# A two-block model kernel: the sum of the down products moved from a VectorE addition to an accumulating transfer

## The chip, the cores and the metric

The kernel runs on one core of a Trainium2 chip, in one launch. The metric is the device time of that core in microseconds, from runs of the whole program.

## What is computed

Two transformer blocks of width 2048 over 256 positions, in float32. The change touches the two feed-forward parts only:

```
# first block (w_up 2048 x 8192, w_down 8192 x 2048)
m = rms_norm(h, mlp_pre_gain[l])
z = jnp.square(jax.nn.relu(jnp.einsum("bsd,df->bsf", m, w_up[l])))
z = jnp.einsum("bsf,fd->bsd", z, w_down[l])
h = h + rms_norm(z, mlp_post_gain[l])
...
# second block (w_gu 2048 x 11264, w_down 5632 x 2048)
h2 = rmsnorm(x, g_ffn)
gu = h2 @ w_gu
x = x + (jax.nn.silu(gu[..., :D_FF_2]) * gu[..., D_FF_2:]) @ w_down
```

## The kernel before

Every large product is cut in units of 512 output columns (W) for all 256 positions, held as two tiles of 128 (TT). A unit sums over 2048 inner rows in eight slots (SPU) of two 128-row pieces each. A slot is one 512 KB piece of weights. It goes through a ring of four (RING): SyncE loads it into `raw`, ScalarE rounds it into `w_hi` (L676), VectorE takes the residue `w_lo` (L976), and TensorE does twelve matmuls of 512 columns with it (L399 to L401: w_lo with x_hi, w_hi with x_hi, w_hi with x_lo) into one of two accumulators `acc`. A ring place is free for ScalarE when TensorE has used it (`slot_used`), and free for SyncE when VectorE has made the residue (`lo_ready`). Each engine's program is written out by hand in one order, and semaphores alone order the engines against each other. The names are the buffers': `ev` (two halves of 512 KB) takes the evacuated accumulator, `wide` (2 MB) is the wide accumulator in SBUF, `zz` holds an activated unit, `b_hi` and `b_lo` its transposed and split form, `h` the residual stream, `ssq` the sums of squares that a norm needs.

The MLP (`mlp_block`) runs four blocks over the inner width. Each has four up units and then four down units (NCH is 4). A down unit j adds its part to `wide[:, :, j]`. In the orders of the engines the boundary of a down unit looks like this. ScalarE has rounded the slots up to four ahead (`ticks`), evacuates `acc` into `ev[:, j % 2]` (`evacuate`, L683), waits for `ev_read`, squares `wide[:, :, j]` for the norm that follows the MLP (`squares`, L709; the squares of the first three blocks are overwritten by those of the fourth), and goes on to the next unit's slots:

```
evacuate(j % 2, g + (NCH + j + 1) * SPU, ev[:, j % 2])
act.wait_ge(ev_read, b * NCH + (4 + j + 1))
squares(3, j, wide[:, :, j], b * (2 * NCH) + (24 + 2 * j))
```

VectorE adds `ev` to `wide` (L1187) when the evacuation is counted in `evacuated` and the squares of the block before are done (`squared`), and counts `ev_read`. After the fourth block come the mean square on VectorE (L1004, L1006), the root on GpSimd (`root`, L1391), the residual (L1147) and the transposes of `h` (L416), on which TensorE's next unit depends.

The second feed-forward (`ff_block`) has two blocks of eight up and four down units, which add into `wide` likewise (L1365), and a third of six up and four down units, in which VectorE adds `wide` to `h` (L1345) and then each down unit to `h` directly (L1362). There ScalarE takes no squares; it waits for `ev_read` only where a half of `ev` is to be written again.

GpSimd clears `wide` before each of the two uses (L1451, L1477), loads gains, tables and attention biases by its own DMA queue, and takes the roots.

Of the kernel before, what the change touches and what calls it, by code (L numbers as in the profile page):

```python
# [21 lines left out]
ALU = mybir.AluOpType  # L22
# [3 lines left out]
D = 2048  # L26
# [3 lines left out]
NCH = D // W  # L30
# [45 lines left out]
def build_program(nc, t):  # L76
    ctx = ExitStack()
    with ctx:
# [9 lines left out]
        def sem(name):  # L88
            return ctx.enter_context(nc.semaphore(name))
# [79 lines left out]
        ev_read = sem("ev_read")  # L169
        x_in = [sem(f"x_in{c}") for c in range(NCH)]  # L170
# [493 lines left out]
        def _(act):  # L664
# [142 lines left out]
            def mlp_block(b, last=False):  # L807
                g = G_MLP + b * (2 * NCH * SPU)
                for j in range(NCH):
                    first = isinstance(b, int) and b + j == 0  # L810
                    ticks(g, RING + j * SPU + (RING if first else 0), RING + (j + 1) * SPU)
                    act.wait_ge(rs_ok, 3)
                    act.wait_ge(z_ready, b * NCH + (4 + j))
                    act.wait_ge(ev_read, b * NCH + 4)
                    evacuate(j % 2, g + (j + 1) * SPU, ev[:, j % 2], 2)
                    split(T_MLP + b * (2 * NCH) + 2 * j, b_hi, 4 * j)
                for j in range(NCH):
                    ticks(g, RING + (NCH + j) * SPU,
                          RING + (NCH + j + 1) * SPU - (last and j == NCH - 1))
                    act.wait_ge(z_ready, b * NCH + 8)  # L820
                    act.wait_ge(ev_read, b * NCH + (4 + j))
                    evacuate(j % 2, g + (NCH + j + 1) * SPU, ev[:, j % 2])
                    act.wait_ge(ev_read, b * NCH + (4 + j + 1))
                    squares(3, j, wide[:, :, j], b * (2 * NCH) + (24 + 2 * j))
# [113 lines left out]
            def ff_block(g, b, pairs, down_slots, last):  # L938
                z, r, tr = 32 + b * NCH, 4 + 16 + b * NCH, T_FF + b * (2 * NCH)
                for j in range(2 * pairs):  # L940
                    ticks(g, RING + j * SPU, RING + (j + 1) * SPU)
                    act.wait_ge(rs_ok, 6)
                    if j % 2 == 0:
                        act.wait_ge(z_ready, z + j // 2)
                        act.wait_ge(ev_read, r)
# [5 lines left out]
                for j in range(NCH):  # L951
# [5 lines left out]
                    if j > 1:  # L957
                        if last:
                            act.wait_ge(h_ready, 3 * NCH + j - 1)
                        else:  # L960
                            act.wait_ge(ev_read, r + (j - 1))
# [9 lines left out]
        def _(dve):  # L971
# [194 lines left out]
            def mlp_block(b, last=False):  # L1166
# [10 lines left out]
                if isinstance(b, int) and b == 0:  # L1177
                    dve.wait_ge(wide_zero, 1)
                for j in range(NCH):
                    ticks(g, RING + (NCH + j) * SPU,  # L1180
                          RING + (NCH + j + 1) * SPU - (last and j == NCH - 1))
                    if last and j:
                        dve.wait_ge(squared, b * (2 * NCH) + (24 + 2 * j))
                        gained(j - 1)
                    dve.wait_ge(evacuated, u + (NCH + j + 1))
                    dve.wait_ge(squared, b * (2 * NCH) + (18 + 2 * j))
                    nc.vector.tensor_tensor(wide[:, :, j], wide[:, :, j], ev[:, j % 2], ALU.add  # L1187
                                            ).then_inc(ev_read, 1)
# [152 lines left out]
            def ff_block(g, u, b, pairs, down_slots, last):  # L1341
                for j in range(2 * pairs):
                    ticks(g, RING + j * SPU, RING + (j + 1) * SPU)
                    if last and 1 <= j <= NCH:
                        nc.vector.tensor_tensor(h[:, :, j - 1], h[:, :, j - 1], wide[:, :, j - 1],  # L1345
                                                ALU.add).then_inc(folded, 1)
# [8 lines left out]
                for j in range(NCH):  # L1355
# [3 lines left out]
                    dve.wait_ge(evacuated, u + (2 * pairs + j + 1))  # L1359
                    if last:  # L1360
                        dve.wait_ge(folded, j + 1)
                        nc.vector.tensor_tensor(h[:, :, j], h[:, :, j], ev[:, j % 2], ALU.add  # L1362
                                                ).then_inc(h_ready, 1)
                    else:
                        nc.vector.tensor_tensor(wide[:, :, j], wide[:, :, j], ev[:, j % 2], ALU.add  # L1365
                                                ).then_inc(ev_read, 1)

            dve.wait_ge(wide_zero, 2)
# [8 lines left out]
        def _(pool):  # L1377
# [76 lines left out]
            root(2)  # L1454
            root(3)
# [22 lines left out]
            root(5)  # L1478

# [45 lines left out]
```

## Time and profile before

| | us |
|---|---|
| median of 2 runs | 2595.22 |
| lowest and highest | 2594.0, 2596.45 |
| span of the profiled execution, first to last instruction | 2592.5 |
| TensorE busy in it | 2533.8 |
| VectorE, ScalarE, GpSimd busy | 1472.3, 1235.2, 245.4 |

The profile is of one execution. Its span leaves out what lies before the first and after the last instruction, so it stands a little under the runs' times. Matmuls are pipelined, so the durations of single ones overlap (0.39 us each at a spacing of 0.23). In the rows PE is TensorE, PEld its weight loads, DVE is VectorE, ACT ScalarE, POOL GpSimd and SP SyncE; "idle before" is how long the engine had nothing to do, and the arrow names what ended that. L and a number is a line of the kernel.

### The profile page before, as it was taken

To read this page: it belongs to the slowest core of one execution; us is meant where nothing else is said; L and a number is where in the kernel's file an instruction comes from. 1 tells how busy PE (TensorE), PEld (TensorE's weight loads), DVE (VectorE), ACT (ScalarE), POOL (GpSimd) and SP (SyncE) were. 2 spreads that over 40 slices of the span, in tenths; PEclk is the share of its full clock that TensorE was granted. 3 is DMA by queue.
4 is the path that set the end of the run, shared out by engine and by line. 5 is a ranking of instruction groups with operands and counts; after the bars stand their busy time and mean duration, and the time that the engine had idled before them with its cause. 6 is when DMAs were issued, how large, how long until landed. Compare 5 with 4: busy or idle time off the path is not lost.

```text
span 2592.5 us, 31914 instructions
## 1 busy us (share of the span) xinstructions
PE 2533.8 (98%) x11389; PEld 2096.6 (81%) x11389; DVE 1472.3 (57%) x1548; ACT 1235.2 (48%) x1509; POOL 245.4 (9%) x199
## 2 busy tenths in 40 slices
PE   8888999999999999989999999999999999999999
PEld 7676778888888888878888888888888888888887
DVE  5899655555545555565566655545545544554554
ACT  5333555444444444454465544444544444444443
POOL 0899200000000000001100000000000000000000
PEclk9999999999999999999999999999999999999999
DMA  7554555565566565545555466665565566565654
GB/s 240 185 153 146 162 171 187 188 194 177 195 189 194 189 190 186 192 145 177 187 188 176 155 203 189 192 194 187 179 195 187 192 193 193 179 198 194 191 188 162
DMA packets 247772, 478.36 MB, mean 185 GB/s; under 512 B 16448, under 2 KB 17016, under 8 KB 247388
## 3 DMA queue, kind: packets, MB, share of 16 engines
q1 hardware_dynamic: 244460, 470.14, 56.8%
q0 software_dynamic: 3152, 6.46, 0.7%
q8 instruction: 85, 1.39, 0.2%
q14 instruction: 43, 0.35, 0.0%
q10 hardware_dynamic: 32, 0.01, 0.0%
HBM read 474.42 MB, written 4.47 MB: 185 GB/s over the span
## 4 chain that ended last, share of the span: by engine, by line
PE 91%; DVE 7%; ACT 1%; DMA 1%; issue 0%; POOL 0%; SPq 0%; ACTq 0%; DVEq 0%
PE acc L399 29%; PE acc L401 29%; PE acc L400 29%; DVE convb L1035 4%; DVE w_lo L976 3%; PE tp L416 2%; DMA raw<-w_in_dram 0%; ACT w_hi L676 0%; PE po L593 0%; DMA h<-x_dram 0%; PE sc L563 0%; DVE h L1147 0%; PE tp L581 0%; PE sc L474 0%; PE po L595 0%
## 5 line engine op out<-in xcount | busy, mean ns | idle before, releaser
L976 DVE TENSOR_TENSOR w_lo<-raw,w_hi 128x1024 fp32r<-128x1024 f32 x888 | 1084.5, 1234 | 927.5 <-ACT w_hi L676 924.0
L676 ACT ACTIVATE w_hi<-raw 128x1024 fp32r<-128x1024 f32 x888 | 930.9, 1060 | 1029.2 <-PE acc L401 960.3
L399 PE MATMUL acc<-w_lo,a_hi 128*128 128x512 f32 x2304 | 910.6, 395 | 11.3 <-DVE w_lo L976 10.6
L400 PE MATMUL acc<-w_hi,a_hi 128*128 128x512 f32 x2304 | 901.1, 391 | 0.0
L401 PE MATMUL acc<-w_hi,a_lo 128*128 128x512 f32 x2304 | 901.1, 391 | 0.0
L399 PEld LDWEIGHTS acc<-w_lo,a_hi 128*128 128x128 f32 x2304 | 435.3, 189 | 109.2 <-DVE w_lo L976 14.7
L401 PEld LDWEIGHTS acc<-w_hi,a_lo 128*128 128x128 f32 x2304 | 434.8, 189 | 91.5
L400 PEld LDWEIGHTS acc<-w_hi,a_hi 128*128 128x128 f32 x2304 | 435.3, 189 | 87.4
L399 PE MATMUL acc<-w_lo,b_hi 128*128 128x512 f32 x1120 | 437.2, 390 | 0.4 <-DVE b_lo L1103 0.4
L401 PE MATMUL acc<-w_hi,b_lo 128*128 128x512 f32 x1120 | 436.3, 390 | 0.0
L400 PE MATMUL acc<-w_hi,b_hi 128*128 128x512 f32 x1120 | 436.3, 390 | 0.0
L399 PEld LDWEIGHTS acc<-w_lo,b_hi 128*128 128x128 f32 x1120 | 210.4, 188 | 44.1 <-DVE b_lo L1103 0.8
L401 PEld LDWEIGHTS acc<-w_hi,b_lo 128*128 128x128 f32 x1120 | 210.4, 188 | 43.5
L400 PEld LDWEIGHTS acc<-w_hi,b_hi 128*128 128x128 f32 x1120 | 210.4, 188 | 43.3
L1391 POOL TENSOR_TENSOR rs<-ms,half 128x2 f32<-128x2 f32 x6 | 4.2, 702 | 1240.2 <-DVE ms L1006 1240.2
L1035 DVE SCALAR_TENSOR_TENSOR convb<-gT,cols,convb 128x256 f32<-128x256 f32 x180 | 114.3, 688 | 0.0
L1419 POOL TENSOR_SCALAR prod<-gT,cols 128x256 f32<-128x256 f32 x60 | 99.4, 1657 | 0.0
L990 DVE TENSOR_TENSOR b_lo<-tp,b_hi 128x512 fp32r<-128x512 f32 x54 | 34.8, 686 | 77.3 <-ACT b_hi L695 77.3
L695 ACT ACTIVATE b_hi<-tp 128x512 fp32r<-128x512 f32 x54 | 29.3, 595 | 98.1 <-PE tp L416 98.1
L686 ACT ACTIVATE ev<-acc,rs 128x512 f32<-128x512 f32 x112 | 69.9, 675 | 0.0
L416 PE MATMUL tp<-ident,zz 128*128 128x128 f32 x344 | 47.4, 283 | 19.6 <-DVE zz L1081 19.6
L416 PEld LDWEIGHTS tp<-ident,zz 128*128 128x128 f32 x344 | 42.0, 146 | 26.1 <-DVE zz L1081 20.8
(155 smaller groups left out, 1007.4 us busy)
## 6 DMA issues: line engine op xcount, KB each, us to landing
raw<-w_in_dram SPq DMA_DIRECT2D x272, 512.0 KB, 3.8
raw<-w_down_dram SPq DMA_DIRECT2D x216, 512.0 KB, 4.7
raw<-w_gu_dram SPq DMA_DIRECT2D x176, 512.0 KB, 4.4
raw<-w_up_dram SPq DMA_DIRECT2D x128, 512.0 KB, 3.7
raw<-w_out_dram SPq DMA_DIRECT2D x64, 512.0 KB, 4.4
raw<-w_branch_dram SPq DMA_DIRECT2D x32, 512.0 KB, 3.6
skew_dram<-line_dram POOLq DMA_DIRECT2D x3, 768.0 KB, 14.1
h<-x_dram SPq DMA_DIRECT2D x4, 512.0 KB, 7.8
```

What stands on the lines that cost most here:

```text
L399: nc.tensor.matmul(out, xh, wl, start=s == 0 and k == 0, stop=False)
L400: nc.tensor.matmul(out, xh, wh, start=False, stop=False)
L401: mm = nc.tensor.matmul(out, xl, wh, start=False, stop=s == n - 1 and k == KS - 1)
L416: tr = nc.tensor.transpose(tp[:, g, (2 * k + tk) * P:(2 * k + tk + 1) * P], src[:, tk, c:c + P], ident[:, :])
L676: nc.scalar.activation(w_hi[:, ring], raw[:, ring], ACT.Copy).then_inc(hi_ready, 1)
L686: a_ = nc.scalar.activation(dst[:, tk], acc[:, pair, tk], func, scale=rs[:, n, tk:tk + 1])
L695: nc.scalar.activation(dst[:, bass.ds(k0 + 2 * g, 2), :].rearrange("p k s -> p (k s)"), tp[:, g, :], ACT.Copy).then_inc(split_hi, 1)
L976: nc.vector.tensor_tensor(w_lo[:, ring], raw[:, ring], w_hi[:, ring].bitcast(F32), ALU.subtract).then_inc(lo_ready, 1)
L990: nc.vector.tensor_tensor(lo_, tp[:, g, :], hi_.bitcast(F32), ALU.subtract).then_inc(split_lo, 1)
L1035: nc.vector.scalar_tensor_tensor(convb[:, c, :], gT[:, c, k:k + S], tap_weight(c, k), convb[:, c, :], ALU.mult, ALU.add).then_inc(conv, 1)
L1391: nc.gpsimd.tensor_tensor(rs[:, n, :], ms[:, n, :], half[:, :], ALU.pow).then_inc(rs_ok, 1)
L1419: nc.gpsimd.tensor_scalar(prod[:, k % 4], gT[:, c, k:k + S], tap_weight(c, k), None, ALU.mult).then_inc(conv_pool, 1)
```

## The change

The 16 additions of the MLP (L1187) and the 8 of the first two blocks of the second feed-forward (L1365) are no longer VectorE instructions. GpSimd issues for each a DMA from `ev[:, j % 2]` to `wide[:, :, j]` that adds to its destination (`accum_op=ALU.add`), after waiting for the evacuation, for the squares of the block before (MLP only) and for the accumulating DMA before it. A new semaphore `summed` goes up by 16 with each that has landed, and takes the place of `ev_read` in ScalarE's waits. VectorE waits for all 24 before it adds `wide` to `h`. GpSimd's new instructions stand between its roots 2 and 3, and after root 5.

```diff
--- before.py
+++ after.py
@@ -167,6 +167,7 @@
         took = sem("took")
         z_ready = sem("z_ready")
         ev_read = sem("ev_read")
+        summed = sem("summed")
         x_in = [sem(f"x_in{c}") for c in range(NCH)]
         ident_in = sem("ident_in")
         pre_in = sem("pre_in")
@@ -811,16 +812,19 @@
                     ticks(g, RING + j * SPU + (RING if first else 0), RING + (j + 1) * SPU)
                     act.wait_ge(rs_ok, 3)
                     act.wait_ge(z_ready, b * NCH + (4 + j))
-                    act.wait_ge(ev_read, b * NCH + 4)
+                    act.wait_ge(ev_read, 4)
+                    if not isinstance(b, int) or b:
+                        act.wait_ge(summed, b * (16 * NCH))
                     evacuate(j % 2, g + (j + 1) * SPU, ev[:, j % 2], 2)
                     split(T_MLP + b * (2 * NCH) + 2 * j, b_hi, 4 * j)
                 for j in range(NCH):
                     ticks(g, RING + (NCH + j) * SPU,
                           RING + (NCH + j + 1) * SPU - (last and j == NCH - 1))
                     act.wait_ge(z_ready, b * NCH + 8)
-                    act.wait_ge(ev_read, b * NCH + (4 + j))
+                    if not isinstance(b, int) or b or j:
+                        act.wait_ge(summed, b * (16 * NCH) + 16 * j)
                     evacuate(j % 2, g + (NCH + j + 1) * SPU, ev[:, j % 2])
-                    act.wait_ge(ev_read, b * NCH + (4 + j + 1))
+                    act.wait_ge(summed, b * (16 * NCH) + 16 * (j + 1))
                     squares(3, j, wide[:, :, j], b * (2 * NCH) + (24 + 2 * j))
 
             mlp_block(0)
@@ -936,13 +940,13 @@
 
 
             def ff_block(g, b, pairs, down_slots, last):
-                z, r, tr = 32 + b * NCH, 4 + 16 + b * NCH, T_FF + b * (2 * NCH)
+                z, r, tr = 32 + b * NCH, b * (16 * NCH) + 16 * 16, T_FF + b * (2 * NCH)
                 for j in range(2 * pairs):
                     ticks(g, RING + j * SPU, RING + (j + 1) * SPU)
                     act.wait_ge(rs_ok, 6)
                     if j % 2 == 0:
                         act.wait_ge(z_ready, z + j // 2)
-                        act.wait_ge(ev_read, r)
+                        act.wait_ge(summed, r)
                     evacuate(j % 2, g + (j + 1) * SPU, ev[:, j % 2], 5,
                              ACT.Copy if j % 2 else ACT.Silu)
                     if j % 2:
@@ -958,7 +962,7 @@
                         if last:
                             act.wait_ge(h_ready, 3 * NCH + j - 1)
                         else:
-                            act.wait_ge(ev_read, r + (j - 1))
+                            act.wait_ge(summed, r + 16 * (j - 1))
                     evacuate(j % 2, g + s0, ev[:, j % 2])
 
             with act.Fori(0, 2) as b:
@@ -1174,18 +1178,12 @@
                     nc.vector.scalar_tensor_tensor(zz[:, :, :], ev[:, j % 2], 0.0, ev[:, j % 2],
                                                    ALU.max, ALU.mult).then_inc(z_ready, 1)
                     split(S_MLP + b * (2 * NCH) + 2 * j, b_hi, b_lo, 4 * j)
-                if isinstance(b, int) and b == 0:
-                    dve.wait_ge(wide_zero, 1)
                 for j in range(NCH):
                     ticks(g, RING + (NCH + j) * SPU,
                           RING + (NCH + j + 1) * SPU - (last and j == NCH - 1))
                     if last and j:
                         dve.wait_ge(squared, b * (2 * NCH) + (24 + 2 * j))
                         gained(j - 1)
-                    dve.wait_ge(evacuated, u + (NCH + j + 1))
-                    dve.wait_ge(squared, b * (2 * NCH) + (18 + 2 * j))
-                    nc.vector.tensor_tensor(wide[:, :, j], wide[:, :, j], ev[:, j % 2], ALU.add
-                                            ).then_inc(ev_read, 1)
 
             mlp_block(0)
             with dve.Fori(1, FF1 // D - 1) as b:
@@ -1342,6 +1340,7 @@
                 for j in range(2 * pairs):
                     ticks(g, RING + j * SPU, RING + (j + 1) * SPU)
                     if last and 1 <= j <= NCH:
+                        dve.wait_ge(summed, 16 * 6 * NCH)
                         nc.vector.tensor_tensor(h[:, :, j - 1], h[:, :, j - 1], wide[:, :, j - 1],
                                                 ALU.add).then_inc(folded, 1)
                     if j % 2 == 0:
@@ -1356,16 +1355,12 @@
                     ticks(g, RING + s0,
                           RING + s0 + down_slots - (RING if last and j == NCH - 1 else 0))
                     s0 += down_slots
-                    dve.wait_ge(evacuated, u + (2 * pairs + j + 1))
                     if last:
+                        dve.wait_ge(evacuated, u + (2 * pairs + j + 1))
                         dve.wait_ge(folded, j + 1)
                         nc.vector.tensor_tensor(h[:, :, j], h[:, :, j], ev[:, j % 2], ALU.add
                                                 ).then_inc(h_ready, 1)
-                    else:
-                        nc.vector.tensor_tensor(wide[:, :, j], wide[:, :, j], ev[:, j % 2], ALU.add
-                                                ).then_inc(ev_read, 1)
-
-            dve.wait_ge(wide_zero, 2)
+
             with dve.Fori(0, 2) as b:
                 ff_block(G_FF + b * (3 * NCH * SPU), U_FF + b * (3 * NCH), b, NCH, SPU, False)
             ff_block(G_FF3, U_FF + 6 * NCH, 2, 3, 6, True)
@@ -1452,6 +1447,20 @@
             pool.dma_start(gain[:, :], bass.AP(t["mlp_post_gain"].tensor, 0, [[0, P], [1, D]])
                            ).then_inc(gain2_in, 16)
             root(2)
+
+            def accumulate(before, u, squared0):
+
+                for j in range(NCH):
+                    pool.wait_ge(evacuated, u + (j + 1))
+                    if squared0 is not None:
+                        pool.wait_ge(squared, squared0 + 2 * j)
+                    if before + j:
+                        pool.wait_ge(summed, before + 16 * j)
+                    pool.dma_start(wide[:, :, j], ev[:, j % 2], accum_op=ALU.add).then_inc(summed, 16)
+
+            pool.wait_ge(wide_zero, 1)
+            for b in range(FF1 // D):
+                accumulate(b * (16 * NCH), U_MLP + NCH + b * (2 * NCH), b * (2 * NCH) + 18)
             root(3)
             root(4)
             with pool.Fori(0, NCH) as i:
@@ -1476,6 +1485,9 @@
             pool.wait_ge(evacuated, U_B0 + 1)
             nc.gpsimd.memset(wide[:, :, :, :], 0.0).then_inc(wide_zero, 1)
             root(5)
+            pool.wait_ge(wide_zero, 2)
+            for b in range(2):
+                accumulate(b * (16 * NCH) + 16 * 16, U_FF + 2 * NCH + b * (3 * NCH), None)
 
 
 def tables():
```

ScalarE at the boundary of a down unit in the first MLP block, before: w_hi is the rounding of a slot, ev<-acc the evacuation, junk,ssq<-wide the squares.

```order
L676 ACTIVATE w_hi<-raw 128x1024 [waits slot_used,landed3]
L683 ACTIVATE ev<-acc 128x1024 [waits slot_used,ev_read,z_ready]
L709 ACTIVATE junk,ssq<-wide 128x512 [waits squared,ev_read]
L709 ACTIVATE junk,ssq<-wide 128x512 [waits squared]
L676 ACTIVATE w_hi<-raw 128x1024 [waits slot_used,landed0]
```

The same place after the change.

```order
L677 ACTIVATE w_hi<-raw 128x1024 [waits slot_used,landed3]
L684 ACTIVATE ev<-acc 128x1024 [waits slot_used,summed,z_ready]
L710 ACTIVATE junk,ssq<-wide 128x512 [waits squared,summed]
L710 ACTIVATE junk,ssq<-wide 128x512 [waits squared]
L677 ACTIVATE w_hi<-raw 128x1024 [waits slot_used,landed0]
```

The instructions stand in the same order; the squares' wait, ahead of all the next unit's slots, is on the landing (`summed`) where it was on VectorE's count (`ev_read`).

VectorE from the fourth up unit of the first MLP block to the second down unit, before: w_lo is the residue of a slot, zz<-ev the activation, b_lo the split of its transpose.

```order
L976 TENSOR_TENSOR w_lo<-raw,w_hi 128x1024 [waits hi_ready] x8
L1174 SCALAR_TENSOR_TENSOR zz<-ev 128x1024 [waits turned,evacuated]
L990 TENSOR_TENSOR b_lo<-tp,b_hi 128x512 [waits split_hi] x2
L976 TENSOR_TENSOR w_lo<-raw,w_hi 128x1024 [waits hi_ready,wide_zero]
L976 TENSOR_TENSOR w_lo<-raw,w_hi 128x1024 [waits hi_ready] x7
L1187 TENSOR_TENSOR wide<-wide,ev 128x2x512 [waits squared,evacuated]
L976 TENSOR_TENSOR w_lo<-raw,w_hi 128x1024 [waits hi_ready] x8
L1187 TENSOR_TENSOR wide<-wide,ev 128x2x512 [waits squared,evacuated]
L976 TENSOR_TENSOR w_lo<-raw,w_hi 128x1024 [waits hi_ready] x8
```

The same place after the change, to the end of the block.

```order
L980 TENSOR_TENSOR w_lo<-raw,w_hi 128x1024 [waits hi_ready] x8
L1178 SCALAR_TENSOR_TENSOR zz<-ev 128x1024 [waits turned,evacuated]
L994 TENSOR_TENSOR b_lo<-tp,b_hi 128x512 [waits split_hi] x2
L980 TENSOR_TENSOR w_lo<-raw,w_hi 128x1024 [waits hi_ready] x32
L1189 UNCONDITIONAL_BRANCH
```

The additions to `wide` have gone from between the residues; 32 residues stand in a row, and the wait for the cleared `wide` has gone to GpSimd.

GpSimd around the MLP, before: rs<-ms,half is a root.

```order
L1451 MEMSET wide 128x4096 [waits h_ready]
L1452 DMA gain<-mlp_post_gain_dram 128x2048
L1391 TENSOR_TENSOR rs<-ms,half 128x2 [waits ssum] x3
L1457 UNCONDITIONAL_BRANCH
L1457 ISA
```

GpSimd there after the change.

```order
L1446 MEMSET wide 128x4096 [waits h_ready]
L1447 DMA gain<-mlp_post_gain_dram 128x2048
L1386 TENSOR_TENSOR rs<-ms,half 128x2 [waits ssum]
L1459 DMA wide<-ev 128x2x512 [waits squared,evacuated,wide_zero]
L1459 DMA wide<-ev 128x2x512 [waits summed,squared,evacuated] x15
L1386 TENSOR_TENSOR rs<-ms,half 128x2 [waits ssum] x2
```

Sixteen DMAs stand between the third and the fourth root; each but the first waits for the one before it to land.

## Rows read from the trace of the kernel before

**Rows 1.** Page: busy us of each engine (share, instructions); chain that ended last, by engine.

```profile
PE 2533.8 (98%) x11389; PEld 2096.6 (81%) x11389; DVE 1472.3 (57%) x1548; ACT 1235.2 (48%) x1509; POOL 245.4 (9%) x199
...
PE 91%; DVE 7%; ACT 1%; DMA 1%; issue 0%; POOL 0%; SPq 0%; ACTq 0%; DVEq 0%
```

**Rows 2.** Windows: stretch, length, busy PE, PEld, DVE, ACT, POOL, PEclk, DMA share, GB/s.

```profile
460.00:1100.00 640.00, 639.39 (x2876) 530.26 (x2875) 332.77 (x290) 302.23 (x360) 0.00 (x0) 1.00 0.59 190
...
2000.00:2592.00 592.00, 586.93 (x2622) 486.64 (x2620) 295.64 (x252) 261.90 (x273) 0.00 (x0) 1.00 0.59 188
```

**Rows 3.** Waits (us in total, times, longest): whole span, then 440 to 1100 us twice.

```profile
PE acc L399 <- DVE w_lo L976: 10.6, 14, 2.9
...
PE acc L399 <- issue: 0.6, 2, 0.3
...
ACT w_hi L676 <- DMA raw<-w_down_dram: 2.2, 1, 2.2
```

**Rows 4.** Timeline of ACT, 503 to 512 us: start us, us, what [idle before <-releaser].

```profile
503.70 1.06 ACT L676 ACTIVATE w_hi<-raw 128x1024 fp32r<-128x1024 f32 x1 [1.66 <-PE acc L401]
504.66 1.01 ACT L683 ACTIVATE ev<-acc 128x1024 f32<-128x1024 f32 x1
507.19 0.63 ACT L709 ACTIVATE junk<-wide 128x512 bf16<-128x512 f32 x1 [1.51 <-DVE wide L1187]
...
508.43 1.99 ACT L676 ACTIVATE w_hi<-raw 128x1024 fp32r<-128x1024 f32 x2
```

**Rows 5.** Timeline of DVE, the same stretch.

```profile
505.93 1.22 DVE L1187 TENSOR_TENSOR wide<-wide,ev 128x1024 f32<-128x1024 f32 x1
509.50 2.36 DVE L976 TENSOR_TENSOR w_lo<-raw,w_hi 128x1024 fp32r<-128x1024 f32 x2 [2.35 <-ACT w_hi L676]
```

**Rows 6.** Timeline of PEld (weight loads), the same stretch.

```profile
503.22 0.19 PEld L399 LDWEIGHTS acc<-w_lo,b_hi 128*128 128x128 f32 x1
...
514.10 0.19 PEld L399 LDWEIGHTS acc<-w_lo,b_hi 128*128 128x128 f32 x1
```

**Rows 7.** Timelines of ACT, POOL and PE at the end of the last MLP block.

```profile
1103.35 1.02 ACT L683 ACTIVATE ev<-acc 128x1024 f32<-128x1024 f32 x1 [1.68 <-PE acc L401]
1105.66 0.63 ACT L709 ACTIVATE junk<-wide 128x512 bf16<-128x512 f32 x1 [1.29 <-DVE wide L1187]
...
1107.47 0.69 POOL L1391 TENSOR_TENSOR rs<-ms,half 128x2 f32<-128x2 f32 x1 [696.29 <-DVE ms L1006]
...
1109.67 1.97 PE L416 MATMUL tp<-ident,h 128*128 128x128 f32 x8 [6.44 <-DVE h L1147]
```

**Rows 8.** Timeline of DVE in the second feed-forward.

```profile
2390.65 1.22 DVE L1365 TENSOR_TENSOR wide<-wide,ev 128x1024 f32<-128x1024 f32 x1
...
2434.23 1.22 DVE L1345 TENSOR_TENSOR h<-h,wide 128x1024 f32<-128x1024 f32 x1
```

**Rows 9.** Issues: KB each, us to landing; then POOL's issues, duration ns min/median/max.

```profile
raw<-w_down_dram SPq DMA_DIRECT2D x216, 512.0 KB, 4.7
...
raw<-w_up_dram SPq DMA_DIRECT2D x128, 512.0 KB, 3.7
...
skew_dram<-line_dram POOLq DMA_DIRECT2D x3, 768.0 KB, 14.1
...
past<-past_dram POOLq DMA_DIRECT2D x1, 128.0 KB, 2.4
...
L1468 POOL DMA_DIRECT2D past<-past_dram x1: 543/543/543, 1316.6 to 1316.6; - x1
...
L1402 POOL DMA_DIRECT2D skew_dram<-line_dram x3: 1080/1096/1153, 45.7 to 72.7; - x3
```

**Rows 10.** PE's clock after an idle time: window (columns as in rows 2), then timelines of PE.

```profile
1109.00:1117.00 8.00, 5.96 (x22) 5.11 (x23) 8.00 (x14) 3.35 (x8) 0.00 (x0) 0.50 0.10 21
...
1121.45 1.03 PE L416 MATMUL tp<-ident,h 128*128 128x128 f32 x8
...
107.08 0.47 PE L399 MATMUL acc<-w_lo,a_hi 128*128 128x512 f32 x1 [0.65 <-DVE w_lo L976]
```

## The prediction

> **What bounds the kernel now.** I read the busy shares first: TensorE is busy 98% of the span, VectorE 57%, GpSimd 9% [rows 1]. The chain that ended last gives 91% to TensorE [rows 1]. So only what stops TensorE counts. The windows then say where it stops: from 460 to 1100 us (three and a half of the four MLP blocks) it is busy 639.39 of 640 us at full clock, and from 2000 us to the end 586.93 of 592 [rows 2]. In all its span TensorE idles 2592.5 - 2533.8 = 58.7 us, so even taking every gap away could barely exceed 2% (51.9 us), about what a measurement of this kernel can tell from no change. The list of waits names where VectorE's late residues stop matmuls: 10.6 us in 14 waits [rows 3], but the same list of 440 to 1100 us has only one entry for TensorE, 0.6 us of issue [rows 3]. In the stages of the change, VectorE's additions cost TensorE nothing.
>
> The third reading is the handover at a unit's end, which the reader is to see in the three timelines of the down product that ends near 503.6 us. ScalarE rounds a weight slot (503.70), evacuates the accumulator (504.66 to 505.67), idles 1.51 us for the addition, squares the sum, and only at 508.43 rounds the next slots [rows 4]. The addition runs 505.93 to 507.15 and the residue of the next slot ends at 509.50 + 1.23 = 510.73 [rows 5]. TensorE's last weight load of this unit's slot is followed by the next unit's first at 503.22, and four ring slots later, at 514.10, it needs that residue [rows 6]: a slot is (514.10 - 503.22)/4 = 2.72 us, and the residue has 514.10 - 510.73 = 3.37 us to spare.
>
> **The change part by part.** Removed: 24 additions of 1.22 us [rows 5], 16 in the MLP, 8 in the second feed-forward, 29.3 us of VectorE. Their cover is TensorE's own matmuls: gain 0, by the windows above.
>
> Added: 24 accumulating transfers of 512 KB issued by GpSimd. Nothing waits on GpSimd's queue behind them that was not later anyway: the next root (1107.47 us [rows 7]) itself needs the last squares. But in the MLP, ScalarE waits for the landing at once, and behind that wait stand the squares and then every w_hi of the next unit; VectorE's residues and TensorE stand behind those. Call R the time from the end of the evacuation to the start of the squares. Before it is 507.19 - 505.67 = 1.52 us [rows 4]. TensorE starts to stall at R = 1.52 + 3.37 = 4.89 us; beyond it each microsecond is TensorE's, since the next slots' raws are already there and rounding a slot (1.06) and its residue (1.23) are both quicker than 2.72, so the ring refills but the loss stays. That holds for 15 of the 16 MLP units. The sixteenth has no matmuls beside it: evacuation ends at 1104.37, squares begin at 1105.66, R = 1.29, and root, residual and transposes hang on it, TensorE being idle 6.44 us already [rows 7]. There all of R - 1.29 is lost. Sum: 15 (R - 4.89) + (R - 1.29) = 16 R - 74.6.
>
> In the second feed-forward ScalarE asks for the sum two units later (43.5 us at 8 slots of 2.72), or, at the next block's first evacuation, one unit later (21.8 us); VectorE folds wide at 2434.2 where the last addition started at 2390.7 [rows 8]. Cost 0 while R is under 21.8.
>
> **The size of R.** No accumulating transfer is in this trace, so I bound it. Below: the plain loads of 512 KB land in 3.7 to 4.7 us, and GpSimd's 128 KB load in 2.4 [rows 9]; with the 0.26 us that VectorE needed after the evacuation (505.67 to 505.93), R = 4.0 at the least. Above: the nearest row of GpSimd that reads and writes about as many bytes on one side, skew_dram<-line_dram, 768 KB, landed in 14.1 us [rows 9], so R = 14.4. Between: an accumulate reads two streams and writes one. Take 2.4 as the part that doesn't grow, and 4.7 - 2.4 = 2.3 for one stream of 512 KB beside the weight loads (the engines are 0.59 busy there [rows 2]); two streams make 7.0, plus 0.26 of semaphore, 0.2 for twice as many rows to describe (GpSimd spent 0.54 us on 128 rows and 1.10 on 512 [rows 9]) and 0.1 for the wake-up: 7.6. Scaled from the other row, 2.4 + 11.7 x 512/768 + 0.5 = 10.7. I take 8.5, nearer to the loads, which write the same 2 KB rows in SBUF, with something for the addition inside the transfer. Then 16 x 8.5 - 74.6 = 61.4 us. Against the profiled span: 2592.5 + 61.4 = 2653.9; the shown runs' median, 2595.22, lies 2.7 us above that span, so 2656.6, rounded to 2656, or 2.3% slower.
>
> The Trainium skill (DMA: Bandwidth & Descriptors, section Anatomy of one DMA) fits GpSimd's transfers as 2.0 us plus bytes over 436 GB/s. Its fixed part agrees with the 2.4 us row. An estimate from it for 512 KB is 3.2 us, which would put R near 3.5 and the cost of the change at 2 us: it would make rival B the outcome. It doesn't say what an accumulate does to the second term.
>
> **Rivals.**
> A, the forecast: R between 7 and 10, 16 R - 74.6 = 37 to 85 us, time 2633 to 2681.
>
> B, the other side: not slower. The transfer is about as fast as a plain one and the ring's spare 4.89 us swallow it in 15 of 16 places. At R = 4.0 only the last unit pays, 2.7 us: 2598. At R = 5.5, 13.4 us: 2609; up to R = 7. For it: 3.7 us loads, and after the unit's end the ring is full, so that few weight loads compete. Against it: twice the bytes are read. The sum crosses 2% at R = (51.9 + 74.6)/16 = 7.9; below that it isn't measurably slower.
>
> C, the transfer is slow and the clock falls. R over 10 stops TensorE over 5 us per unit. After an idle of 6.44 us the trace shows eight transposes in 1.97 us [rows 7] instead of 1.03 and a granted clock of 0.50, the lower of its levels (1.2 GHz), from 1109 to 1117 us, while the matmul after an idle of 0.65 us takes 0.47 us [rows 10]. Half clock for that stretch's some 7 us costs 3.4 us of work a time. At R = 12: 117.4 + 15 x 3.4 = 168, time 2764; at R = 14.4, 2802. For it: the skew row, and the addition inside the transfer has no row at all. Against: the loads' rows.
>
> D, weight loads are held back. A load issued when a residue ends at 506.0 lands by 510.7 and is needed at 503.70 + 4 x 2.72 = 514.6, 3.9 us later. If all 4.6 us of an accumulate's two streams went ahead of it, 0.7 us would be late, in both stages: 24 x 0.7 = 17 us on top of the forecast, 2673. The one wait for w_down in the MLP is 2.2 us [rows 3], so there is room.
> The Trainium skill (same page, section Issuing engines are not separate DMA queues) says that transfers of all engines interleave on the same 16 DMA engines; that is this rival's mechanism, and no row here prices it for an accumulate.
>
> E, the change does nothing for the time: VectorE's relief meets no wait and the landing is quick, 2595; a gain of over 2% would need nearly all of TensorE's 58.7 idle us.
>
> **How the numbers follow.** A 0.45, B 0.30, C 0.18, D 0.04, E 0.03. Slower by over 2% (above 2647): C, D and two thirds or so of A, those with R over 7.9: 0.54. Within 2%: B, nearly all of E and the rest of A: 0.44. Faster by over 2%: 0.02. The range runs from B's lower end, 2598, to C at R = 12, 2765, and leaves out the far part of C and E's other side. The forecast's own range is 2633 to 2681. The likeliest case gives the time: 2656.
>
> **What would show it.** Right: ScalarE's wait before the squares of wide grows from 1.5 to about 8.3 us, 16 times, released by a transfer; TensorE shows 15 new waits of some 3.6 us for w_lo in the MLP and none in the second feed-forward; the gap at 1103 us grows by 7; 24 transfers stand in GpSimd's row of issues with 7 to 8 us to landing; VectorE's busy time falls by 29 us and buys nothing. Wrong in size: landing under 5 us (B) or over 10 (C, with stretches of granted clock 0.5 inside the MLP). Wrong in mechanism: TensorE's new waits stand in the second feed-forward, or ScalarE's w_hi waits for raw (D), or TensorE stalls although R stays under 4.9.

## The result

The changed kernel takes 2667.97 us (median of 2 runs, 2664.76 to 2671.18) where the kernel before took 2595.22. The ratio is 1.027, with a 95% interval of 1.0231 to 1.0308: slower by 72.8 us. The forecast was 2656 us. The profiled execution's span is 2663.0 us, 70.5 longer than before.

The page of the changed kernel, for the row of busy times and the chain in [rows 1]:

```profile
PE 2557.3 (96%) x11389; PEld 2108.4 (79%) x11389; DVE 1442.3 (54%) x1524; ACT 1231.5 (46%) x1509; POOL 274.5 (10%) x223
...
PE 81%; DVE 8%; issue 5%; DMA 4%; ACT 2%; ACTq 0%; POOL 0%; SPq 0%; DVEq 0%
```

VectorE is busy 30 us less (1442.3 for 1472.3). TensorE's work is the same 11,389 matmuls, yet its busy time rose by 23.5 us; and 4% of the chain that ended last is now a transfer from `ev` to `wide`. The windows show in which stage it went; they answer to [rows 2].

```profile
460.00:1100.00 640.00, 605.34 (x2657) 496.58 (x2656) 285.23 (x252) 272.39 (x326) 15.66 (x13) 0.98 0.61 184
...
2050.00:2663.00 613.00, 607.37 (x2716) 503.38 (x2714) 296.39 (x253) 271.18 (x283) 9.62 (x8) 1.00 0.64 195
```

In 640 us of the MLP TensorE is busy 605.34 us (before 639.39), at a granted clock of 0.98. The second feed-forward, with its 8 accumulating transfers, is what it was: 607.37 of 613 us busy, 5.6 us idle against 5.1 of before. The waits, for [rows 3]: first of the whole span, then TensorE's from 440 to 1180 us, which hold the MLP.

```profile
ACT junk L710 <- DMA wide<-ev: 128.2, 16, 8.9
...
PE acc L400 <- DVE w_lo L980: 52.9, 28, 3.7
...
PE acc L400 <- DVE w_lo L980: 42.5, 15, 3.7
PE tp L417 <- DVE h L1151: 10.5, 1, 10.5
```

ScalarE waits 16 times for a landing, 128.2 us in all. TensorE has 15 new waits for a residue, 42.5 us, and the one gap at the end of the MLP is 10.5 us where it was 6.44. How one of them comes about is in the timelines of ScalarE and TensorE around the first down unit, for [rows 4] and [rows 6]:

```profile
506.72 1.01 ACT L684 ACTIVATE ev<-acc 128x1024 f32<-128x1024 f32 x1
516.63 0.63 ACT L710 ACTIVATE junk<-wide 128x512 bf16<-128x512 f32 x1 [8.90 <-DMA wide<-ev]
...
520.23 0.79 PE L400 MATMUL acc<-w_lo,b_hi 128*128 128x512 f32 x1 [3.69 <-DVE w_lo L980]
520.82 0.63 PE L401 MATMUL acc<-w_hi,b_hi 128*128 128x512 f32 x1
...
526.50 0.39 PE L400 MATMUL acc<-w_lo,b_hi 128*128 128x512 f32 x1
```

The evacuation ends at 507.73, and the squares begin 8.90 us later. TensorE has by then used its four slots, stands idle 3.69 us, and comes back at half speed: its matmuls last 0.63 us and follow each other at 0.43 until 526, then 0.39 at 0.23 again. The granted clock of the 7 us from 520 is 0.56, half speed until 526 and full after it, and 1.00 in the 7 us behind them (columns as in [rows 2]):

```profile
520.00:527.00 7.00, 6.78 (x18) 5.35 (x19) 3.68 (x5) 2.81 (x3) 0.00 (x0) 0.56 0.72 224
527.00:534.00 7.00, 7.00 (x33) 5.79 (x32) 3.58 (x3) 2.12 (x2) 0.00 (x0) 1.00 0.64 209
```

The issues and the landing, for [rows 9]:

```profile
raw<-w_down_dram SPq DMA_DIRECT2D x216, 512.0 KB, 4.8
...
wide<-ev POOLq DMA_DIRECT2D x24, 512.0 KB, 8.2
...
L1459 POOL DMA_DIRECT2D wide<-ev x24: 1191/1200/1287, 508.3 to 2461.1; - x24
...
DMA to landing us min/median/max: 5.0/8.2/10.3
```

An accumulating transfer of 512 KB lands in 8.2 us (median), 5.0 at the quickest, and GpSimd takes 1.2 us to issue it. Loads of w_down take 4.8 us, before 4.7.

The profiled difference adds up: the waits for residues in the MLP 42.5, the gap at its end 10.5 - 6.4 = 4.1, TensorE's longer busy time 23.5, together 70.1 of 70.5 us. Not all of the 23.5 is the clock. The 15 stalls should be 15 x (8.19 - 4.89) = 49.5 us long by the prediction's sum (8.19 us is the mean wait of these 15 units), and the idle column shows 42.5; the 7.0 between them stand in the busy time too, as matmuls on either side of a stall that last longer. The rest is 16.5.

### The profile page after: what moved, and what is told of

The parts are those of the page before. It is cut to its first block, busy times and chain, and to the rows that moved or that the text cites. A ratio compares the mean times of both kernels' runs of the same rounds, so it can differ in the third digit from the quotient of the medians.

```text
span 2663.0 us, 31923 instructions
## 1 busy us (share of the span) xinstructions
PE 2557.3 (96%) x11389; PEld 2108.4 (79%) x11389; DVE 1442.3 (54%) x1524; ACT 1231.5 (46%) x1509; POOL 274.5 (10%) x223
## 4 chain that ended last, share of the span: by engine, by line
PE 81%; DVE 8%; issue 5%; DMA 4%; ACT 2%; ACTq 0%; POOL 0%; SPq 0%; DVEq 0%
PE acc L400 26%; PE acc L402 26%; PE acc L401 26%; DVE convb L1039 4%; DMA wide<-ev 4%; DVE w_lo L980 3%; PE tp L417 2%; ACT w_hi L677 1%; ACT ev L684 1%; ACT junk L710 0%; DMA raw<-w_in_dram 0%; PE po L594 0%; PE sc L564 0%; DMA h<-x_dram 0%; DVE h L1151 0%
## 5 line engine op out<-in xcount | busy, mean ns | idle before, releaser
L400 PE MATMUL acc<-w_lo,b_hi 128*128 128x512 f32 x1120 | 445.7, 398 | 38.3 <-DVE w_lo L980 37.9
L401 PE MATMUL acc<-w_hi,b_hi 128*128 128x512 f32 x1120 | 442.3, 395 | 0.0
L402 PE MATMUL acc<-w_hi,b_lo 128*128 128x512 f32 x1120 | 441.8, 394 | 0.0
L1459 POOL DMA_DIRECT2D wide<-ev x24 | 28.9, 1203 | 1254.6 <-ACT ev L684 965.6
L710 ACT ACTIVATE junk<-wide 128x512 bf16<-128x512 f32 x32 | 19.9, 622 | 128.2 <-DMA wide<-ev 128.2
L994 DVE TENSOR_TENSOR b_lo<-tp,b_hi 128x512 fp32r<-128x512 f32 x54 | 34.8, 686 | 77.5 <-ACT b_hi L696 77.5
```

What stands on the lines that cost most here:

```text
L400: nc.tensor.matmul(out, xh, wl, start=s == 0 and k == 0, stop=False)
L401: nc.tensor.matmul(out, xh, wh, start=False, stop=False)
L402: mm = nc.tensor.matmul(out, xl, wh, start=False, stop=s == n - 1 and k == KS - 1)
L994: nc.vector.tensor_tensor(lo_, tp[:, g, :], hi_.bitcast(F32), ALU.subtract).then_inc(split_lo, 1)
L1459: pool.dma_start(wide[:, :, j], ev[:, j % 2], accum_op=ALU.add).then_inc(summed, 16)
```

## The experiments

Theory 1 is the prediction's: in the MLP ScalarE waits for each landing ahead of the next unit's slots, TensorE stalls for what exceeds the ring's spare time, and the stalls let its clock fall. Theory 2: the traffic of the transfers holds back weight loads. Theory 3: the loss lies in the transfer or in GpSimd's queue, wherever ScalarE waits. All ratios are to the kernel before, on the same chip.

### Which of the two stages, and is it the wait?

**e1_mlp_only** is the changed kernel with VectorE's additions put back in the second feed-forward:

```diff
-                            act.wait_ge(summed, r + 16 * (j - 1))
+                            act.wait_ge(ev_read, r + (j - 1))
...
+                        nc.vector.tensor_tensor(wide[:, :, j], wide[:, :, j], ev[:, j % 2], ALU.add
+                                                ).then_inc(ev_read, 1)
```

> Only the 16 additions of the MLP are accumulating transfers; the 8 of the second feed-forward are VectorE additions again. Theory 1 (ScalarE waits for each landing ahead of the next unit's slots, in the MLP alone; TensorE stalls for what exceeds the ring's spare time, and the stalls let its clock fall): the whole loss stays, 2668 us, ratio 1.027. Theory 2 (the transfers' traffic holds back weight loads wherever they run): a third of the transfers is gone, so about a third of the 73 us comes back, 2644 us.

Measured: 2664.05 us, ratio 1.0265 (1.0246 to 1.0284). The whole loss is there, as far as the interval tells.

**e2_ff_only** has them put back in the MLP instead:

```diff
-                    act.wait_ge(summed, b * (16 * NCH) + 16 * (j + 1))
+                    act.wait_ge(ev_read, b * NCH + (4 + j + 1))
...
+                    nc.vector.tensor_tensor(wide[:, :, j], wide[:, :, j], ev[:, j % 2], ALU.add
+                                            ).then_inc(ev_read, 1)
```

> The other half: only the 8 sums of the second feed-forward are accumulating transfers (ScalarE's two blocks there are written out rather than looped, which changes no order). Theory 1: nothing waits for them within 21 us, so 2595 us, ratio 1.000, with no wait of TensorE in that stage. Theory 2: 8 of 24 transfers cost a third, 2619 us.

Measured: 2594.82 us, ratio 1.0004 (0.9987 to 1.0022). Its list of waits and its issues:

```profile
ACT junk L710 <- DVE wide L1189: 26.7, 16, 2.6
...
PE acc L400 <- DVE w_lo L978: 9.5, 13, 2.9
...
raw<-w_gu_dram SPq DMA_DIRECT2D x176, 512.0 KB, 4.3
...
wide<-ev POOLq DMA_DIRECT2D x8, 512.0 KB, 8.6
```

Eight transfers that took 8.6 us each cost nothing, because nobody asks for them for 21 us. TensorE's waits for residues are 9.5 us in 13, those of [rows 3]. A landing time is no cost by itself.

**e3_pause_memset** is the kernel before, with no accumulating transfer at all, in which ScalarE also waits for a memset on GpSimd:

```diff
                     act.wait_ge(ev_read, b * NCH + (4 + j + 1))
+                    act.wait_ge(paused, b * NCH + (j + 1))
...
+                pool.wait_ge(evacuated, U_MLP + NCH + b * (2 * NCH) + j + 1)
...
+                nc.gpsimd.memset(qkT[:, 0:16, :], 0.0)
+                nc.gpsimd.memset(qkT[:, 16:32, :], 0.0).then_inc(paused, 1)
```

> The kernel before, with its VectorE additions and no accumulating transfer; ScalarE's wait before the squares in the MLP is lengthened to about 7.4 us (0.26 of semaphore and 7.05 of GpSimd's memset of a 32 KB scratch per partition, which starts at the same evacuation). Theory 1: the wait alone makes the loss: 15 x (7.4 - 4.89) + (7.4 - 1.3) = 44 us, and the fallen clock some 10 to 20 more, so 2640 to 2660 us. Theory 2: no transfer, no loss, 2595 us.

Measured: 2637.14 us, ratio 1.0159 (1.0142 to 1.0176). A wait with no transfer behind it makes the loss. ScalarE's timeline around the first two down units, and TensorE's waits in the MLP:

```profile
511.64 0.63 ACT L710 ACTIVATE junk<-wide 128x512 bf16<-128x512 f32 x1 [7.12 <-issue]
...
535.70 0.63 ACT L710 ACTIVATE junk<-wide 128x512 bf16<-128x512 f32 x1 [7.13 <-issue]
...
PE acc L400 <- DVE w_lo L978: 25.7, 15, 2.0
PE tp L417 <- DVE h L1149: 12.3, 1, 12.3
```

The wait is 7.13 us. A unit takes 535.70 - 511.64 = 24.06 us from squares to squares, where eight slots of 2.72 are 21.76: 2.3 us lost, and 7.13 - 4.89 = 2.24 was the sum's. TensorE's idle column shows less, 25.7/15 = 1.7, since the matmuls on either side of a stall last longer; that part stands in its busy time. Theory 2 said 2595. One part of my expectation did not come: the sum's 44 us are about what was lost (42), and the 10 to 20 us for the clock, which made it 2640 to 2660, are not there.

**e4_no_wait_012** keeps all 24 transfers, but in three of four MLP blocks ScalarE squares a piece of `h`, whose sum nothing uses:

```diff
-                    act.wait_ge(summed, b * (16 * NCH) + 16 * (j + 1))
-                    squares(3, j, wide[:, :, j], b * (2 * NCH) + (24 + 2 * j))
+                    if last:
+                        act.wait_ge(summed, b * (16 * NCH) + 16 * (j + 1))
+                    squares(3, j, (wide if last else h)[:, :, j], b * (2 * NCH) + (24 + 2 * j))
```

> The changed kernel, all 24 transfers kept; in MLP blocks 0 to 2 ScalarE squares a piece of h in place of wide (those sums of squares are overwritten by block 3 and used by nothing), so that it doesn't wait for 12 of the 16 landings. Theory 1: only block 3 pays, 3 x 3.1 + 4 to 6.7, and 5 to 10 for the clock: 2613 to 2621 us. Theory 2: same traffic, same loss, 2668 us.

Measured: 2613.13 us, ratio 1.0064 (1.0046 to 1.0082). The same traffic with 12 of 16 waits gone loses 17.7 of the 72.8 us. Theory 2 has fallen in four runs.

### Where the wait stands

**e5_late_1** and **e6_late_4** move the wait and the squares behind one and behind four slots of the next unit. K is 1 or 4; the squares of a block's last unit go behind the first slots of the next block in the same way, and only the very last unit's stay where they were:

```diff
                 for j in range(NCH):
...
+                    s0 = RING + (NCH + j) * SPU
+                    if j:
+                        ticks(g, s0, s0 + K)
+                        act.wait_ge(summed, b * (16 * NCH) + 16 * j)
+                        squares(3, j - 1, wide[:, :, j - 1], b * (2 * NCH) + (22 + 2 * j))
+                        s0 = s0 + K
```

> The changed kernel, same transfers and same squares of wide, but ScalarE rounds one slot of the next unit before it waits for the landing and squares (all units but the very last). Theory 1 (the wait costs what exceeds the ring's spare time at its place in ScalarE's order): the spare time grows from 4.89 by a slot of 2.72 to 7.61 us. The 15 waits of the changed kernel were 7.5 to 8.9 us, so 0 to 1.3 us of each is left, 8 to 12 us in all, plus 4 us at the last unit, where TensorE's gap grew from 6.4 to 10.5 us: 2605 to 2612 us, hardly any time at the low clock in the MLP. Theory 3 (the loss lies in the transfer itself, its traffic or GpSimd's queue, not in where ScalarE waits): 2668 us.

Measured: 2624.64 us, ratio 1.0106 (1.0088 to 1.0123). Most of the loss is gone, so theory 3 has fallen, but 28 us are left where 9 to 16 were expected. ScalarE's timeline says why:

```profile
505.14 1.01 ACT L684 ACTIVATE ev<-acc 128x1024 f32<-128x1024 f32 x1
506.89 1.06 ACT L677 ACTIVATE w_hi<-raw 128x1024 fp32r<-128x1024 f32 x1 [0.74 <-PE acc L402]
515.79 0.63 ACT L710 ACTIVATE junk<-wide 128x512 bf16<-128x512 f32 x1 [7.83 <-DMA wide<-ev]
...
PE acc L400 <- DVE w_lo L992: 15.4, 13, 1.8
...
wide<-ev POOLq DMA_DIRECT2D x16, 512.0 KB, 8.7
```

Seen from the end of the evacuation (506.15), the squares start 9.6 us later, not 8.9. The landing has itself become slower: 8.7 us (median in the MLP) where the changed kernel has 7.9 there. A part of that is scatter, since e1, whose MLP is the changed kernel's, has 8.3; the means of the 16 landings are 8.4 against 7.6 and 7.7. I had moved the wait and taken the landing as fixed. The slot rounded earlier gives its raw buffer back earlier, and one more weight load runs beside the transfer; that this load is the cause fits the trace, but wasn't separated. The median unit so exceeds 7.61 by over 1 us; TensorE waits 15.4 us for residues in the MLP, the gap at its end adds 5.0 (11.4), and its busy time is 7.5 us longer.

> As the one before, with four slots rounded ahead of the wait (10.9 us more to spare, 15.8 in all). Theory 1: every landing is hidden, no stall in the MLP but at the last unit, 4 us and a little clock there: 2599 to 2602 us. Theory 3: 2668 us.

Measured: 2599.18 us, ratio 1.001 (1.0001 to 1.002). ScalarE's and TensorE's waits:

```profile
ACT junk L710 <- DMA wide<-ev: 6.1, 1, 6.1
...
PE tp L417 <- DVE h L1163: 11.2, 1, 11.2
...
PE acc L400 <- issue: 0.6, 2, 0.3
```

Of 16 waits one is left, the last unit's of 6.1 us, and TensorE has no wait for a residue in the whole MLP. The transfers, which here have a median of 8.5 us over the span, are hidden.

**e11_late_4_last_dve** adds the very last unit's sum on VectorE, on top of e6:

```diff
-                        act.wait_ge(summed, b * (16 * NCH) + 16 * (j + 1))
+                        act.wait_ge(ev_read, 5)
...
+                if last:
+                    dve.wait_ge(evacuated, u + 2 * NCH)
...
+                    nc.vector.tensor_tensor(wide[:, :, 3], wide[:, :, 3], ev[:, 1], ALU.add
+                                            ).then_inc(ev_read, 1)
```

> e6_late_4 (squares behind four slots of the next unit) with the very last MLP unit's sum added by VectorE, as in the kernel before: 23 accumulating transfers. Theory 1: the 4 us that were left at the last unit go too, and no term remains: 2595 to 2596 us, ratio 1.000, TensorE's gap at the end of the MLP back at 6.4 us. It can't beat the kernel before, since VectorE's relief of 28 us meets no wait.

Measured: 2595.22 us, ratio 0.9995 (0.9978 to 1.0013). No term of the sum is left, and nothing is won either: 23 additions off VectorE are worth nothing in this kernel. The list of waits of the whole span has TensorE's gaps for `h` back at those of before (before 11.7 us in 2, longest 6.4):

```profile
PE tp L417 <- DVE h L1163: 11.7, 2, 6.5
```

### How the loss depends on the wait

**e9_pause_short** and **e10_pause_long** are e3 with another memset, `qkT[:, 0:21]` for the short one, and a third memset of `qkT[:, 0:16]` for the long one:

```diff
-                nc.gpsimd.memset(qkT[:, 0:16, :], 0.0)
-                nc.gpsimd.memset(qkT[:, 16:32, :], 0.0).then_inc(paused, 1)
+                nc.gpsimd.memset(qkT[:, 0:21, :], 0.0).then_inc(paused, 1)
```

> As e3_pause_memset (VectorE adds, no transfer), with GpSimd's memset shortened to 128x5376, 0.86 ns an element, 4.6 us: a wait of 4.7 us, three times that of the kernel before, but under the 4.89 us that the ring has to spare. Theory 1: no stall at the 15 units, only 4.7 - 1.3 = 3.4 us at the last one: 2599 us, ratio 1.001. If the spare time was misread and each microsecond of the wait counts, 16 x (4.7 - 1.5) = 51 us, 2646 us.

Measured: 2600.55 us, ratio 1.0019 (1.0002 to 1.0035).

> As e3_pause_memset, with the memset half as long again (128x12288, 10.6 us): a wait of 10.7 us. Stalls of 5.8 us at 15 units are 87 us and the last unit adds 9.4. Theory 1 without a clock term: 2595 + 96 = 2691 us. With it (each long stall costs a stretch at half clock, up to 3.4 us of work each time): up to 51 more, 2720 to 2742 us, and a stretch of low clock behind nearly every one of the 15 stalls.

Measured: 2721.1 us, ratio 1.0476 (1.0443 to 1.0509). One wait of ScalarE of each kernel, and TensorE's waits for residues in the MLP, first of e9, then of e10:

```profile
531.54 0.63 ACT L710 ACTIVATE junk<-wide 128x512 bf16<-128x512 f32 x1 [4.73 <-issue]
...
PE acc L400 <- DVE w_lo L978: 0.9, 1, 0.9
```

```profile
545.99 0.63 ACT L710 ACTIVATE junk<-wide 128x512 bf16<-128x512 f32 x1 [10.70 <-issue]
...
PE acc L400 <- DVE w_lo L978: 81.0, 15, 5.5
...
PE 2571.3 (95%) x11389; PEld 2118.4 (78%) x11389; DVE 1468.4 (54%) x1548; ACT 1231.4 (45%) x1509; POOL 414.4 (15%) x247
```

With a wait of 4.73 us there is no stall worth the name (0.9 us); with one of 10.70 us all 15 units stall. The knee lies where the prediction put it, and above it the clock comes on top:

| wait (us) | kernel | 16 R - 74.6 | measured in the profiled span | beyond the sum | mean granted clock |
|---|---|---|---|---|---|
| 1.67 (mean of 16) | before | | 0 | | 0.991 |
| 4.73 | e9 | last unit only, 3.4 | 3.4 | 0 | 0.991 |
| 7.13 | e3 | 39.5 | 42.2 | 2.7 | 0.988 |
| 8.01 (mean of 16) | changed | 53.6 | 70.5 | 16.9 | 0.982 |
| 10.70 | e10 | 96.6 | 127.2 | 30.6 | 0.973 |

Each line is one profiled execution, and the runs of the kernel before differ among themselves by 5 us and more, so the 2.7 us of e3 can't be told from nothing by the table alone. The 16.9 and 30.6 are larger, and the busy times agree with them: in the changed kernel 16.5 us, as worked out above, and in e10 TensorE is busy 37.5 us longer than before (2571.3 for 2533.8), of which 15 x 5.81 - 81.0 = 6.2 are the hidden part of the stalls.

The time spent at half clock is twice the missing clock: 2 x 0.018 x 2663.0 = 96 us in the changed kernel and 2 x 0.009 x 2592.5 = 47 before; half of the difference, some 25 us, bounds the work lost to it, and 16.9 are found. Stalls read off TensorE's idle column as up to 2.0 us (e3) cost next to nothing so, those of 1.0 to 3.7 us (changed) about 1.1 us each, those of 4.5 to 5.5 us (e10) 2.0 each. The traces' record of the granted clock shows it as a matter of how often: a stretch at half clock follows 3 of the 15 stalls in e3, 8 of 15 in the changed kernel and in e1, and all 15 in e10. The length of the stall alone doesn't decide it. In the changed kernel none follows three stalls of 3.0 to 3.3 us (idle until 575, 716 and 937 us), and one follows each of two shorter ones, of 2.3 and 2.9 us (767 and 962).

### What of the transfer's time is the addition, and what the size

**e7_half_size** and **e8_plain_copy** change the one line that issues:

```diff
-                    pool.dma_start(wide[:, :, j], ev[:, j % 2], accum_op=ALU.add).then_inc(summed, 16)
+                    pool.dma_start(wide[:, 0, j], ev[:, j % 2, 0], accum_op=ALU.add).then_inc(summed, 16)
```

```diff
-                    pool.dma_start(wide[:, :, j], ev[:, j % 2], accum_op=ALU.add).then_inc(summed, 16)
+                    pool.dma_start(wide[:, :, j], ev[:, j % 2]).then_inc(summed, 16)
```

> The changed kernel with every transfer halved: only the first 128 positions are accumulated (128x512, 256 KB), the sum of the other 128 is left out. The landing beside weight loads took 8.2 us for 512 KB; with 2.4 us that don't grow, half gives 5.3, so a wait of 5.4: Theory 1: 15 x 0.5 + 2.6 = 10 us, 2605 us. If the time is mostly the same for 256 KB (descriptors or the fixed part rule), the wait stays near 8 us and so does the loss, 2660 us.

> The changed kernel with the same 24 transfers of 512 KB from ev to wide by GpSimd, but plain copies without the addition (so wide holds the last unit's part, not the sum). It measures what the accumulation itself adds. Theory 1a (an accumulate is two streams): the growing part halves, 2.4 + 5.8/2 = 5.3 us to landing, a wait of 5.4, 2605 us. Theory 1b (a SBUF to SBUF transfer issued by GpSimd is as slow without the addition): wait 8 us, 2665 us.

Measured: half the size 2628.81 us, ratio 1.0135 (1.0102 to 1.0167); plain copy 2635.09 us, ratio 1.0135 (1.0113 to 1.0157); the medians alone are 1.0125 and 1.0149 times that of before. Both lie between their two expectations. ScalarE's 16 waits are 107.4 and 108.6 us, for which 16 R - 74.6 gives 33 and 34 us; by the medians 32 and 39 were lost. In e8's profiled run some 3 us more than before are a stall of 6.3 us near 272 us, ahead of the first transfer, where before had 2.9. GpSimd's issues and the landings, of e7, then of e8:

```profile
L1459 POOL DMA_DIRECT2D wide<-ev x24: 850/859/945, 506.4 to 2426.0; - x24
...
DMA to landing us min/median/max: 4.2/6.5/7.2
```

```profile
L1459 POOL DMA_DIRECT2D wide<-ev x24: 722/722/761, 511.2 to 2433.1; - x24
...
DMA to landing us min/median/max: 4.1/6.6/7.3
```

Half the bytes, or no addition, take the landing from 8.2 to 6.5 or 6.6 us, not to 5.3. GpSimd's own time is 0.72 us for a plain copy, 0.86 for half an accumulate, 1.20 for a whole one, and it stands at the head of each landing time.

The quickest landing of each kernel is the last unit's of the MLP, when the ring is nearly full and the weight loads run out. They have not quite ended, though. In e8 the transfer is issued at 1143.6 us, and one more weight load, issued at 1142.0, lands 4.5 us later, at 1146.5:

```profile
L278 SPq DMA_DIRECT2D raw<-w_in_dram x1: 373/373/373, 1142.0 to 1142.0; - x1
...
DMA to landing us min/median/max: 4.5/4.5/4.5
```

The last unit's transfer of seven traces, in us after its issue:

| kernel | transfer | last weight load lands | transfer lands |
|---|---|---|---|
| changed | whole accumulate | 2.0 | 5.0 |
| e1 | whole accumulate | 2.4 | 5.3 |
| e4, e6 | whole accumulate | 2.9, 2.9 | 5.7, 5.7 |
| e5 | whole accumulate | 3.4 | 5.9 |
| e7 | half accumulate | 2.8 | 4.2 |
| e8 | plain copy | 2.9 | 4.1 |

The longer a weight load runs beside the accumulate, the later it lands, and 2 to 3 of the 8.2 us go with the stream of weight loads. That they come from sharing the DMA engines fits this but was only argued, since TensorE, VectorE and ScalarE stand idle at that place too. No run has a transfer alone, and what it would take there is open. The addition costs 1.6 us both in the stream (8.2 for 6.6) and at the end of the MLP, where kernels with the same overlap are compared (5.7 for 4.1). Of it 0.48 us is GpSimd's longer issue.

## Why the prediction was right

**What bounds.** Right. The windows and the waits placed every gain at zero, and e11 shows it: 23 additions less, ratio 0.9995.

**Where the loss arises.** Right, step by step. The wait ahead of the next unit's slots makes it (e3, with no transfer), its place in ScalarE's order decides (e6), in the MLP alone (e1, e2), at 15 units plus the last one. The 4.89 us to spare, worked out from six rows of one handover, hold between 4.73 (no stall) and 7.13 us (2.3 us a unit).

**The second feed-forward.** Right: predicted 0, measured 1.0004.

**The size of R.** I took 8.5 us, a pick between the two estimates of 7.6 and 10.7; the mean over the 16 is 128.2/16 = 8.01. The 15 units beside weight loads take (128.2 - 5.3)/15 = 8.2, the last one 5.34. The number came out well by a composition that was wrong in each part: I put a plain transfer at 4.7, but GpSimd's plain copy takes 6.6; I put a second stream at 2.3 and the addition costs 1.6; GpSimd's issue takes 1.2 and not 0.7. And I used one R for the last unit, which stood in my own sum as having no matmuls beside it: it has hardly any weight load beside it either, so its term is 5.34 - 1.29 = 4.1 and not 7.2.

**The clock.** Here the forecast's sum was short. With the measured waits it gives 16 x 8.01 - 74.6 = 53.6 us, and 70.5 were measured in the profiled spans. I had priced the clock only in rival C, for stalls of 5 us and more, because the rows showed a stall of 6.44 us that dropped it and one of 0.65 us that didn't, and set the price to 0 at a stall of 3.6. The changed kernel's first stall, 3.69 us, was followed by matmuls at half speed for over 5 us. Between two rows that far apart the term should have been a range, 0 to 3.4 us at each of 15 units, and not nothing: 0 to 51 us on top of the sum. That 2656 came within 12 us of 2668 is in part luck: R was too large by 7.8 us in the sum (61.4 for 53.6), and the clock, left out, was 16.9 the other way.

**The signs.** ScalarE's wait before the squares was to grow to 8.3 us and grew to 8.0, 16 times; 15 waits for a residue in the MLP were to be some 3.6 us each and are 42.5/15 = 2.8 in the idle column; the gap at the MLP's end was to grow by 7 us and grew by 4.1; VectorE's busy time was to fall by 29 and fell by 30.

**The rivals.** B fell because the landing was 8.2 us. The fit of the Trainium skill (DMA: Bandwidth & Descriptors, section Anatomy of one DMA), which spoke for it with an estimate of 3.2 us for 512 KB, is below both plain cases measured: 6.6 us in the stream of weight loads, and 4.1 at the end of the MLP, where a weight load was still landing. No run here has a transfer with no load beside it. C's mechanism, the clock, joined A's at smaller stalls; its condition, R over 10, wasn't met. D: ScalarE's waits for w_down did grow (15.2 us in 9, from 2.2), but they do so without any transfer as well (25.3 us in 13 in e3, 34.8 in 17 in e9), and are gone with all the transfers in e6 (2.0 in 1). They come with ScalarE's wait, after which the ring has to refill, not with the traffic; and since TensorE hardly stalls in e9, they cost nothing there by themselves.

## What to carry to other kernels

Moving an operation to an engine that is free saves nothing unless the old one stood on the path, and where an engine waits for it at once it costs what its latency grows beyond the time to spare (here 4.89 us). Look for what stands behind that wait in the waiting engine's order: here the squares, which only the norm after the last block needs, held back all the weight roundings, and moving them four slots later hid landings of 8.5 us entirely at 15 of the 16 units. Work out the spare time from one handover's rows, test it with an artificial wait on either side, and give a stall of TensorE of some 2 us or more a range above its own length.

## What of the hardware was unexpected

- An accumulating transfer of 512 KB from SBUF to SBUF, issued by GpSimd, landed in 8.2 us (median) beside a weight stream and in 5.0 to 5.9 where the last weight load ended 2.0 to 3.4 us after the issue; the same as a plain copy in 6.6 and 4.1, half of it in 6.5 and 4.2. Halving it took away 1.5 to 1.7 us, less than the 2 to 3 us that the end of the weight stream did.
- GpSimd needed 1.20 us to issue the whole accumulate, 0.86 for half its rows and 0.72 for a plain copy of all of them; 128 rows of a plain load took 0.54 [rows 9].
- A TensorE stall of 3.69 us was enough for half clock afterwards, in a stream that had been at full clock. The low stretches didn't follow every stall of that size: they followed 8 of 15 stalls of 1.0 to 3.7 us, which cost 16.9 us beyond their length, and 15 of 15 of 4.5 to 5.5 us, which cost 30.6.
- The same wait moved by one slot made the landing slower (8.7 us in the MLP for 7.9 and 8.3 in two traces without the move): a latency measured at one place in the stream isn't a constant of the transfer.
